# Own rows of each expert loaded by SyncE on the hardware queue, in place of a gather by index on GpSimd

## The reference

```
u = rms_norm(x) ; P = u @ W_in                          # columns split into groups
A = stick-breaking attention, 8 heads of 64 ; G = gated linear attention, 4 heads
h = x + concat(A, G) @ W_out
v = rms_norm(h)
group = argmax(v @ W_grp + b_grp)                       # 1 of 4 groups
e1, e2 = top 2 of the group's 8 experts by v @ W_exp + b_exp
h = h + sum over the two of gate(e) * (silu(v @ Wg[e]) * (v @ Wu[e])) @ Wd[e]
```

## Time and profile before

| | |
|---|---|
| median of 3 runs | 1253.36 us (1251.5 to 1255.86) |
| the profiled execution | 1249.58 us, span 1247.7 us |
| mean granted TensorE clock | 0.982 |
| TensorE matmuls busy | 1178.1 us (94%) |
| VectorE, ScalarE busy | 869.1 us (70%), 734.4 us (59%) |
| GpSimd busy | 272.6 us (22%) |
| HBM | 242.79 MB read, 48.25 MB written |
| chain that ended last | PE 33%, DMA 16%, DVE 6%, ACT 3%, issue 2% |

### The profile page before, as it was taken

How to read it: one execution, slowest core, us unless ns; L and a number is a source line. 1 busy time by engine, 2 the same in 40 slices (tenths; PEclk the granted TensorE clock), 3 DMA queues, 4 the chain that set the end, 5 groups by cost and what they waited for, 6 DMA issues and landing times.

```text
span 1247.7 us, 17672 instructions
## 1 busy us (share of the span) xinstructions
PE 1178.1 (94%) x6172; PEld 964.4 (77%) x6172; DVE 869.1 (70%) x991; ACT 734.4 (59%) x894; POOL 272.6 (22%) x249
## 2 busy tenths in 40 slices
PE   5999999999999997999997999999999999999993
PEld 4897787877777765777786888888888878888882
DVE  6721112276556696687778989998888888888981
ACT  5532222366454593222356888887777877878870
POOL 3300000010000001233241333343443332232210
PEclk9999999999999998999988999999999999999997
DMA  8155523020000132375679999999999999999971
GB/s 260 44 203 185 182 113 110 1 69 18 18 18 17 50 129 77 128 252 207 241 274 353 359 377 375 384 371 372 374 383 374 373 378 380 372 379 391 381 251 16
DMA packets 67828, 288.12 MB, mean 231 GB/s; under 512 B 13008, under 2 KB 20193, under 8 KB 43202
## 3 DMA queue, kind: packets, MB, share of 16 engines
q1 hardware_dynamic: 51538, 238.30, 50.5%
q0 software_dynamic: 10864, 30.29, 8.9%
q10 hardware_dynamic: 5376, 18.88, 3.9%
HBM read 242.79 MB, written 48.25 MB: 233 GB/s over the span
## 4 chain that ended last, share of the span: by engine, by line
PE 33%; DMA 16%; DVE 6%; ACT 3%; issue 2%; POOL 0%; ACTq 0%; POOLq 0%; DVEq 0%
DMA raw<-in_expert_w_up 16%; PE banks L742 9%; PE banks L744 9%; PE banks L743 9%; DVE ew_l L1556 3%; ACT ew_h L1384 2%; PE banks L1079 1%; PE banks L987 1%; PE banks L1108 1%; PE banks L911 1%; PE banks L1059 1%; PE banks L924 1%; DVE r_small L1764 1%; PE banks L978 0%; PE banks L1052 0%
## 5 line engine op out<-in xcount | busy, mean ns | idle before, releaser
L1556 DVE TENSOR_TENSOR ew_l<-raw,ew_h 128x2048 fp32r<-128x2048 f32 x192 | 438.0, 2290 | 63.3 <-ACT ew_h L1384 62.1
L1384 ACT ACTIVATE ew_h<-raw 128x2048 fp32r<-128x2048 f32 x192 | 368.3, 1919 | 119.8 <-PE banks L744 59.7
L742 PE MATMUL banks<-ew_h,xb_h 128*128 128x512 f32 x512 | 203.9, 398 | 8.4 <-issue 4.1
L744 PE MATMUL banks<-ew_h,xb_l 128*128 128x512 f32 x512 | 200.7, 392 | 0.0
L743 PE MATMUL banks<-ew_l,xb_h 128*128 128x512 f32 x512 | 200.5, 392 | 0.0
L1682 DVE TENSOR_TENSOR_SCAN tails<-tails 128x512 f32<-128x512 f32 (+3 forms) x96 | 94.0, 1021 | 62.8 <-ACT tails L1350 62.5
L742 PE MATMUL banks<-win_h,u_h 128*128 128x512 f32 (+1 forms) x320 | 122.5, 383 | 2.8 <-DVE u_l L1556 2.5
L742 PEld LDWEIGHTS banks<-ew_h,xb_h 128*128 128x128 f32 x512 | 97.1, 190 | 30.0 <-issue 10.4
L743 PE MATMUL banks<-win_l,u_h 128*128 128x512 f32 (+1 forms) x320 | 118.8, 371 | 0.0
L744 PE MATMUL banks<-win_h,u_l 128*128 128x512 f32 (+1 forms) x320 | 118.8, 371 | 0.0
L744 PEld LDWEIGHTS banks<-ew_h,xb_l 128*128 128x128 f32 x512 | 96.8, 189 | 20.7
(11 more groups left out here) (242 smaller groups left out, 1993.9 us busy)
## 6 DMA issues: line engine op xcount, KB each, us to landing
raw<-in_expert_w_gate SPq DMA_DIRECT2D x64, 1024.0 KB, 12.1
raw<-in_expert_w_up SPq DMA_DIRECT2D x64, 1024.0 KB, 13.3
raw<-in_expert_w_down SPq DMA_DIRECT2D x64, 1024.0 KB, 12.6
rows_dram<-zero_rows ACTq DMA_DIRECT2D x8, 2048.0 KB, 7.6
win_raw<-in_w_in SPq DMA_DIRECT2D x16, 512.0 KB, 5.5
x_in<-in_x SPq DMA_DIRECT2D x8, 512.0 KB, 10.6
raw<-in_w_out SPq DMA_DIRECT2D x4, 1024.0 KB, 5.4
h_row<-in_x SPq DMA_DIRECT2D x8, 512.0 KB, 6.6
```

Source lines behind the costliest of these rows:

```text
L742: mm(ps, lh, rh, start=start, stop=False)
L744: return mm(ps, ll, rh, start=False, stop=stop)
L1384: A(ew_h[slot % SPLIT][:, :], raw[raw_slot][:, :], ACT.Copy).then_inc(ew_h_ready, 1)
L1556: return V.tensor_tensor(dst, src, high.bitcast(fp32), SUB)
```

## The change

SyncE loads the rows of blocks 2 to 31 straight from the expert's own slots: 64, 96 or 128 contiguous rows by class, in front of the fifth piece of each expert's turn. It waits for the transposes of the block before (`x_turned`) and for the control words, and reads the class. A new semaphore, `own_in`, tells TensorE. GpSimd gathers only extra blocks, and after each adds 16 to `own_in` itself, so that the count goes on. In the first turns GpSimd only scatters, and the gathers of blocks 2 and 3 ahead of them are gone. VectorE no longer marks the empty slots. The loads of blocks 0 and 1 stay. A slot that holds no row now arrives as zeros, where before it was left out.

```diff
@@ -263,6 +263,7 @@
         wo_in = [sem(f"wo_loaded{i}") for i in range(2)]
         wo_h_ready, wo_l_ready = sem("wo_h_ready"), sem("wo_l_ready")
         first_half = sem("first_half")
+        own_in = sem("own_rows_in")
         gv_loaded, gate_loaded = [sem(f"gv_loaded{i}") for i in range(2)], sem("gate_loaded")
         g_kv, g_state, g_o, g_sq, g_ms, g_rs, g_normed = (sem("g_kv"), sem("g_state"), sem("g_o"), sem("g_sq"), sem("g_ms"),
                                                          sem("g_rs"), sem("g_normed"))
@@ -470,8 +471,27 @@
             for j in range(2, 6):
                 sp_e.wait_ge(ew_l_ready, j - 1)
                 load_piece(raw_slot(4 + j), gate_up(1, j) if j < 4 else down_v[0][:, PIECE * (j - 4):PIECE * (j - 3)])
+            own_v = own_dram.rearrange("(e p) d -> e p d", p=P)
+
+            def own_rows(i):
+                def move(n):
+                    sp_e.dma_start(xb[0:n, :], own_v[bass.ds(i, 1), 0:n, :].rearrange("e p d -> p (e d)")).then_inc(own_in, 16)
+
+                sp_e.wait_ge(x_turned, i)
+                sp_e.wait_ge(control_ready, 1)
+                size = sp_e.value_load(control[0:1, bass.ds(i + 18, 1)], min_val=0, max_val=2)
+                with sp_e.If(size > 1):
+                    move(MOVED[2])
+                with sp_e.Else():
+                    with sp_e.If(size > 0):
+                        move(MOVED[1])
+                    with sp_e.Else():
+                        move(MOVED[0])
+
             for m in range(10, 22):
                 i, j = (m + 2) // 6, (m + 2) % 6
+                if j == 4:
+                    own_rows(i)
                 if m == 12:
                     sp_e.wait_ge(x_turned, 1)
                     for k in range(2):
@@ -483,8 +503,10 @@
                 load_piece(raw_slot(m), gate_up(i, j) if j < 4 else down_v[i - 1][:, PIECE * (j - 4):PIECE * (j - 3)])
 
 
-            def expert_pieces(i, e, before_e):
+            def expert_pieces(i, e, before_e, own=False):
                 for j in range(6):
+                    if own and j == 4:
+                        own_rows(i)
                     sp_e.wait_ge(ew_l_ready, 6 * i + j - 7)
                     if j < 4:
                         v = (gate_v, up_v)[j // 2]
@@ -494,7 +516,7 @@
                     sp_e.dma_start(raw[j][:, :], src.rearrange("e p n -> p (e n)")).then_inc(raw_in[j], 16)
 
             with sp_e.Fori(4, EXPERTS) as i:
-                expert_pieces(i, i, i - 1)
+                expert_pieces(i, i, i - 1, own=True)
             sp_e.wait_ge(control_ready, 1)
             blocks = sp_e.value_load(control[0:1, 0:1], min_val=0, max_val=MAX_BLOCKS - 1 - EXPERTS) + EXPERTS
             with sp_e.If(blocks > EXPERTS):
@@ -675,7 +697,7 @@
 
             def gather(i):
                 nc.gpsimd.tensor_copy(gather_idx[:, :], source[:, bass.ds(i, 1)]).then_inc(idx_ready, 1)
-                held(idx_ready, i - 1)
+                held(idx_ready, i - EXPERTS + 1)
 
                 def move(n):
                     pool.indirect_dma_start(out=xb[0:n, :], out_offset=None, in_=rows_dram,
@@ -694,22 +716,22 @@
                 by_size(i, move)
 
             pool.wait_ge(control_ready, 1)
-            pool.wait_ge(x_turned, 2)
-            gather(2)
             pool.wait_ge(given_scattered, 32 * TILES)
             nc.gpsimd.dma_start(table[:, 0:EXPERTS, :], table_dram[0:EXPERTS * P, :].rearrange("(p e) c -> p e c", e=EXPERTS)).then_inc(
                 table_in, 16)
             pool.wait_ge(table_in, 16)
             rows(0)
-            pool.wait_ge(x_turned, 3)
-            gather(3)
+
             pool.wait_ge(y_ready, 1)
             scatter(0)
             blocks = pool.value_load(control[0:1, 0:1], min_val=0, max_val=MAX_BLOCKS - 1 - EXPERTS) + EXPERTS
 
-            def turn_over(i):
-                held(x_turned, i + 2)
-                gather(i + 2)
+            def turn_over(i, fetch=None):
+                if fetch is not None:
+                    held(x_turned, i + 2)
+                    fetch(i + 2)
+                    held(rows_in, 16 * (i + 5 - EXPERTS))
+                    nc.gpsimd.memset(gather_idx[:, :], 0).then_inc(own_in, 16)
                 held(y_added, 16 * (i - 1))
                 rows(i - 1)
                 held(y_ready, i)
@@ -724,8 +746,11 @@
             pool.wait_ge(extra_in, 16 * EXTRA)
             link(nc.gpsimd.tensor_scalar(source[:, EXPERTS:MAX_BLOCKS].bitcast(i32), table[:, EXPERTS:MAX_BLOCKS, 0].bitcast(i32),
                                          float(EXPERTS * P), None, ADD))
-            with pool.Fori(2 + EXTRA, blocks - 2) as i:
+            with pool.Fori(2 + EXTRA, EXPERTS - 2) as i:
                 turn_over(i)
+            with pool.If(blocks > EXPERTS):
+                with pool.Fori(EXPERTS - 2, blocks - 2) as i:
+                    turn_over(i, gather)
             for back in (3, 2, 1):
                 held(y_added, 16 * (blocks - back))
                 rows(blocks - back)
@@ -1073,7 +1098,10 @@
             add_rows(TILES - 1, 1).then_inc(x_turned, 1)
 
             def turn_rows(i):
-                pe.wait_ge(rows_in, 16 * (i + 1))
+                if isinstance(i, int) and i < 2:
+                    pe.wait_ge(rows_in, 16 * (i + 1))
+                else:
+                    pe.wait_ge(own_in, 16 * (i - 1))
                 rows = xb[:, :].rearrange("p (d k) -> p k d", k=KT)
                 for k in range(KT):
                     last = nc.tensor.transpose(bank[k // 4][:, P * (k % 4):P * (k % 4 + 1)], rows[:, k, :], ident[:, :])
@@ -1890,10 +1918,7 @@
                 link(V.reduce_sum(ctl_f[:, 2:18], product, axis=AX.X))
                 V.tensor_copy(ctl_f[:, 0:1], end_extra[:, EXPERTS - 1:EXPERTS])
                 link(V.tensor_scalar(ctl_f[:, 2:18], ctl_f[:, 2:18], float(EXPERTS - 1), None, ALU.min))
-                V.tensor_scalar(empty[:, :], counts, slot[:, 0:1], FAR, ALU.is_le, MUL)
-                link(V.tensor_copy(control[:, :], ctl_f[:, :]))
-                V.tensor_tensor(source[:, 0:EXPERTS].bitcast(i32), source[:, 0:EXPERTS].bitcast(i32), empty[:, :], ADD).then_inc(
-                    control_ready, 1)
+                V.tensor_copy(control[:, :], ctl_f[:, :]).then_inc(control_ready, 1)
 
             def find_extra():
                 link(V.tensor_tensor(before_v, product, per_row(n_extra[:, :], EXPERTS, EXTRA), MUL))
```

## The result

The changed kernel took 1285.72 us (median of 4 runs, 1280.88 to 1291.21) against 1252.51 us (1251.5 to 1255.86) for the kernel before in the same comparison: a ratio of 1.0264, 95% interval 1.0238 to 1.029. I had forecast 1245 us, and nothing above 1265 in any rival. The profiled execution took 1280.88 us, span 1279.1 us.

A forecast was written before the change was run, and what follows sets the result against it. In the expert stage TensorE's 17.75 us an expert was its own pace, DMA supply the later bound at 17.98; -7.3 - 0.4 = -7.7 us from the 1253.36 median gave 1245.7, stated as 1245, range 1239 to 1258.

The forecast's parts named there:

- (a): Expert stage: own loads at 0.77 us replace gathers at 1.65 us, supply is never late, 7.3 us come back.
- my upper end of 2.01: Highest price in us of an expert's own load: 78.9 rows at a gather's price per row, 25.5 ns.
- the balance of 17.98 against 17.75 us: Expert stage before the change: time per expert that the DMA engines need, against TensorE's own pace.
- (b): Own load lands behind the expert's fourth piece; costs nothing with supply ahead: 0 taken, range 0 to +2.2 us once.
- R1: Rival, slower: a row costs as much DMA time from SP as from POOL; 1259 to 1265 us, chance 0.13.
- (c): SP's added waits, size load, branches and issue, 1.9 us, stay hidden: 0, at most 1.9 us once.
- (d): POOL loses 30 index copies and 30 gathers, time nobody waits for: 0, at best 0.5 us.
- (f): After the last transposes nothing changes.
- (e): VectorE builds no indices for empty slots, so expert 1 starts about 0.4 us earlier; bounds 0 to 0.5 us.
- R2: Rival, no change: own load costs 1.42 to 1.65 us, supply stays the bound; 1250 to 1255 us, chance 0.19.
- R3: Rival, more than forecast: timed executions lose more to supply and all returns; 1242 to 1238 us, chance 0.10.

The follow-up runs named there:

- e3: Changed kernel, but every own load moves all 128 slots, with no class read or branches: 1244.36 us, ratio 0.9939.
- e6: Kernel before the change, but each gather by index always moves all 128 slots and empty slots are not marked: 1243.3 us, ratio 0.9925.
- e9: Changed kernel with 64-row own loads into a spare buffer nobody reads; transposes of blocks 2 to 31 wait for no load: 1284.31 us, ratio 1.0225.
- e11: Changed kernel with own loads by class issued one piece earlier, in front of the fourth piece instead of the fifth: 1294.95 us, ratio 1.0327.
- e7: Changed kernel with own loads by class issued by ScalarE on its own hardware queue, right behind `x_high`: 1251.58 us, ratio 0.9992.
- e1: Changed kernel, but every own load moves 64 rows to partitions 0 to 63 without reading a class; rows beyond 64 left out: 1285.66 us, ratio 1.0255.
- e2: Changed kernel, but every own load moves 64 rows to partitions 32 to 95, the wrong slots: 1243.3 us, ratio 0.9919.
- e10: Changed kernel, but every own load moves 96 rows to partitions 0 to 95, nothing left out: 1288.88 us, ratio 1.0308.

## Why the prediction was wrong

**(a) Rows on SP's queue: the step that failed.** "a load costs 0.323 / 420 = 0.77 us ... because kind, packet and queue are those of rows 8." Measured: 19.29 - 14.94 - 1.39 = 2.96 us, nearly four times that and above my upper end of 2.01. The load of x behind the earlier trace rows writes all 128 partitions; the own load of this change writes 64 or 96 of them, from partition 0. Kind, packet and queue were the same, and the three together do not fix the price. With the partitions of a piece, all 128, the same step gives what I forecast: e3 goes from expert 4 to 31 in 1193.04 - 713.70 = 479.3 us against 1198.67 - 712.03 = 486.6 before, 7.3 us less, the size of the term. So the balance of 17.98 against 17.75 us was right, and its price for the new load was not.

My upper end came from a wrong split too. I read the gather's dips in the earlier trace rows as dead time of the software queue plus bytes, and a row's price from them; e6 has the same queue with twice the rows and no such loss (experts 11 to 31 from 836.60 to 1192.64 us, 17.80 us each). The packet records say it directly: beside a gather of before the weights' packets take 471 and 412 ns in place of 314, and over e6's 850 to 1190 us they average 318. What those rows showed was already the price of a load of 48 to 87 partitions. It had been in the trace of before, under another name.

**(b) Place in the queue.** Wrong as a forecast (13 waits for rows in the later half, 3.2 us at most), but not the cause: e9 has no such wait and takes 1284.31 us, e11 moves the load forward and takes 1294.95. The rows land 14.4 us after their issue, because the whole queue is late. What (b) didn't ask is whether the queue itself matters. It does: the same loads take 1285.72 us on SP's queue, 1256.82 on GpSimd's, 1251.58 on ScalarE's, a load on the last costing 1.77 us and not 2.96. Why a queue shared with the pieces is worse stays open. The Trainium skill's rule that I weighed under R1 ("DMA: Bandwidth & Descriptors", section "Issuing engines are not separate DMA queues"), that moving loads to another issuing engine saves only issue time, does not hold for these loads; the moment of issue moved with the queue, as said under e7.

**(c), (d), (f)**: nothing in the runs speaks against zero. SP's added work is no bound: e1 has neither read nor branches and is as slow, and e3 keeps PE busy throughout.

**(e) VectorE.** Right in its size. Its timeline after:

```profile
652.05 0.20 DVE L1921 CAST control<-ctl_f 128x66 int32<-128x66 f32 x1
652.16 2.28 DVE L1584 TENSOR_TENSOR ew_l<-raw,ew_h 128x2048 fp32r<-128x2048 f32 x1
```

From the last operation on `ctl_f` (L1892 before, L1920 after) to expert 1's matmul it was 663.61 - 650.38 = 13.23 us before and 664.69 - 651.85 = 12.84 after: 0.39 us less. That stretch began 1.5 us later than before in this profile, and in e3's as well (expert 4 at 713.70 against 712.03); what moved it stays open. So expert 1's matmul came at 664.69 us and not at the 663.2 that I had named.

**The rivals.** R1 had the direction and the waits, but not the mechanism: a price per row falls by e2, e3 and e10, and its time, 1265 us at most, by the result. R2 and R3 needed smaller prices. I did not weigh the Trainium skill's "SBUF — State Buffer" (section "Door 1: The DMA port swizzle (why [64,N] ≈ [32,N])"), which points at the partitions. But its figure would not have turned the forecast: at the 218 GB/s that it gives as the limit for partitions 0 to 63, a load of 0.262 MB takes 1.20 us, an estimate, and the need of 17.53 us still lies under PE's 17.75. Measured, such a load costs 3.31 us (e1). The sum failed for want of a row: nothing in the trace of before showed a load of 64 partitions on the hardware queue, and I bounded it by packets and rows, not by place.

## What to carry to other kernels

Where DMA is close to the bound, a load that writes only part of the partitions can cost more than a whole one although it has fewer bytes: before rounding down to what is needed, time it with all 128 partitions, once with each queue. Here the whole load was 41 us faster than half of it (e3 against e1), and rounding the gather of the kernel before up was worth 9.7 us (e6). When a new transfer appears as the wait that ends last, let its result go unused once (e9): if the time stays, what costs is what it does to the queue, and not its lateness.

## What the runs showed of the hardware that I had not expected

- Two loads of 64 partitions each in place of one of 128, equal bytes: 1333.01 against 1244.36 us, (1333.01 - 1244.36) / 30 = 2.96 us for each split, beyond what PE's pace hides.
- 64 rows of 4 KiB at partitions 32 to 95 cost nothing visible and at 0 to 63 42 us; at 2 KiB a row the latter is 1245.5 us.
- A badly placed load is paid by its neighbours: a weight packet of 8 KiB took 488 ns beside it and 309 ns alone (kernel after, 1068 to 1072 and 1195 to 1197 us).
- The DMA share is about 1.0 of all 16 engines in windows of 349 GB/s and of 400 GB/s alike, so it does not tell how much was delivered.
- The same loads by class are 34 us apart between two hardware queues (e7 and the kernel after), with another moment of issue.
